# Block boundaries by halves: sums, spreads, roots and slices in another order, and a tile of weights rounded earlier

## The reference, cut to what matters

```python
# first block, each layer
x = x + rms_norm(m, norm_mix_post[l])          # m = merged @ w_out, the mixer's last product
h = rms_norm(x, norm_ffn_pre[l])
f = (silu(h @ w_gate) * (h @ w_up)) @ w_down
x = x + rms_norm(f, norm_ffn_post[l])
# second block, each layer
x = x + gt1 * (mix @ w_out)
h = rmsnorm(x, g_ffn[l]) * (1 + sc2) + sh2
x = x + gt2 * ((silu(h @ w1) * (h @ w3)) @ w2)
```

## Time and profile before

| | us |
|---|---|
| median of 3 runs | 3113.05 |
| lowest and highest | 3111.66, 3120.28 |
| the profiled execution: its time | 3113.11 |
| its span, first to last instruction | 3111.3 |
| PE busy in it | 3041.8 (98%) |
| PEld, DVE, ACT, POOL busy | 2573.5, 1409.4, 1369.7, 1344.3 |
| mean granted TensorE clock | 0.994 |

### The profile page before, as it was taken

How to read it: one execution, slowest core, us unless ns; L and a number is a source line. 1 busy time by engine, 2 the same in 40 slices (tenths; PEclk the granted TensorE clock), 3 DMA queues, 4 the chain that set the end, 5 groups by cost and what they waited for, 6 DMA issues and landing times. The chain is left out here.

```text
span 3111.3 us, 46651 instructions
## 1 busy us (share of the span) xinstructions
PE 3041.8 (98%) x16812; PEld 2573.5 (83%) x16812; DVE 1409.4 (45%) x2710; ACT 1369.7 (44%) x2215; POOL 1344.3 (43%) x715
## 2 busy tenths in 40 slices
PE   9999999999999999999999999999999999999999
PEld 7788888888887788888888886778888867788888
DVE  5754336555416744445655424953211149532111
ACT  6866554322227765564322224554222245642222
POOL 3333334444453333335344453544444535444454
PEclk9999999999999999999999999999999999999999
DMA  3222223366532122223366523211333332113332
GB/s 134 68 78 92 91 89 115 98 204 202 181 108 77 65 84 84 89 91 135 97 207 197 175 97 104 75 62 55 101 101 108 109 110 69 64 60 101 101 108 101
DMA packets 93609, 333.48 MB, mean 107 GB/s; under 512 B 10864, under 2 KB 12080, under 8 KB 93232
## 3 DMA queue, kind: packets, MB, share of 16 engines
q1 hardware_dynamic: 91760, 325.52, 31.6%
q10 hardware_dynamic: 1728, 6.36, 0.5%
HBM read 329.69 MB, written 8.44 MB: 109 GB/s over the span
## 5 line engine op out<-in xcount | busy, mean ns | idle before, releaser
L462 POOL TENSOR_TENSOR wLo<-wring,wHi 128x1024 fp32r<-128x1024 f32 x466 | 1115.0, 2394 | 1528.9 <-ACT wHi L440 1528.6
L510 PE MATMUL psG<-hHi,wHi 128*128 128x512 f32 (+1 forms) x2960 | 1121.1, 379 | 8.1 <-POOL wLo L462 4.9
L510 PE MATMUL psG<-hLo,wHi 128*128 128x512 f32 (+1 forms) x2960 | 1104.9, 373 | 4.0 <-POOL hLo L595 3.8
L510 PE MATMUL psG<-hHi,wLo 128*128 128x512 f32 (+1 forms) x2960 | 1103.6, 373 | 0.0
L440 ACT ACTIVATE wHi<-wring 128x1024 fp32r<-128x1024 f32 x466 | 491.3, 1055 | 824.7 <-PE psG L510 795.1
L510 PEld LDWEIGHTS psG<-hHi,wHi 128*128 128x128 f32 x2960 | 561.0, 190 | 105.2 <-issue 28.8
L510 PEld LDWEIGHTS psG<-hLo,wHi 128*128 128x128 f32 x2960 | 560.8, 189 | 84.6 <-POOL hLo L595 10.2
L510 PEld LDWEIGHTS psG<-hHi,wLo 128*128 128x128 f32 x2960 | 561.3, 190 | 71.5 <-issue 0.5
L510 PE MATMUL psG<-hidHi,wHi 128*128 128x512 f32 x704 | 267.8, 380 | 0.1
L510 PE MATMUL psG<-hidHi,wLo 128*128 128x512 f32 x704 | 266.8, 379 | 0.0
L510 PE MATMUL psG<-hidLo,wHi 128*128 128x512 f32 x704 | 266.8, 379 | 0.0
(11 more groups left out here) (394 smaller groups left out, 3737.9 us busy)
## 6 DMA issues: line engine op xcount, KB each, us to landing
wring<-in_w SPq DMA_DIRECT2D x474, 512.0 KB, 3.5
modw<-in_wmod SPq DMA_DIRECT2D x96, 512.0 KB, 4.1
head_raw<-in_w SPq DMA_DIRECT2D x16, 512.0 KB, 5.2
e_copies<-e_rows ACTq DMA_DIRECT2D x8, 512.0 KB
T_tab<-e_copies SPq DMA_DIRECT2D x4, 1024.0 KB, 5.4
mask<-in_mask SPq DMA_DIRECT2D x2, 1536.0 KB, 6.0
xin_sb<-in_x SPq DMA_DIRECT2D x4, 512.0 KB, 5.3
e_copies<-e_rows ACTq DMA_DIRECT2D x8, 256.0 KB
```

The source lines that it names most:

```text
L462: pool.tensor_tensor(wLo[:, home(c), :, :], wring[:, home(c), :, :], wHi[:, home(c), :, :], ALU.subtract).then_inc(w_cut[c % RING], 1)
L510: mm = pe.matmul(out, w[:, k, :], r(j), start=start and j == 0 and n == 0, stop=stop and j == len(kts) - 1 and n == 2)
```

## The change

Only the order of steps changes, and three dummy matmuls go. In the first block:

- PE: the spread of N2 for half 0 stands ahead of `out_half(1, 5)`. The spread of N3 for half 0 comes after feature 4 of `out_half(1, 7)` and no longer behind all of it. All sums of N2 for half 1 but the last stand in one group after `out_half(1, 7)`. `keep_awake(pe, 3)` is gone. The spread of N3 for half 1 comes one feature earlier.
- ACT and DVE: two tiles of `normed_half(0)` and `high_half(0)` come before the copy and the square of `out_half(1, 7)`. The root and the inverse of N2 for half 1 come later in their streams, behind tile 4 and tile 5. DVE norms four tiles of half 1, not one, ahead of the first `head_hid`.

In the second block:

- ACT, POOL and SP: chunk `CH2_WR + 1` is rounded behind `out6`, right after chunk `CH2_WR`, and its rest is made ahead of the last kept tile's. The load of chunk `CH2_GU + 1` waits for `out7` itself.
- PE: the sums for half 0 stand in two groups (six tiles, two tiles), no longer one by one between the rest tiles. The last sums of half 1 come after feature 1 of the first SwiGLU tile and not after feature 3, and their spread comes before the second SwiGLU tile.
- DVE: four tiles of half 1 are scaled, not two, ahead of the first `head_hid`.

```diff
@@ first block, PE
                     out_half(1, 4, 4)
-                    out_half(1, 5, 0, 2)
                     half_spread(pe, t_N2[0], 0, 1)
-                    out_half(1, 5, 2)
+                    out_half(1, 5)
                     out_half(1, 6)
                     x_sums_of(0, range(5))
                     out_half(1, 7, 0, 2)
                     x_sums_of(0, range(5, KT))
-                    out_sums(1, range(3, KT - 2))
-                    out_half(1, 7, 2)
+                    out_half(1, 7, 2, 5)
                     half_spread(pe, t_N3[0], 0, 2)
-                    out_sums(1, (KT - 2,))
-                    keep_awake(pe, 3)
+                    out_half(1, 7, 5)
+                    out_sums(1, range(3, KT - 1))
                     head(0, 0, 0, 0, 2, h_done(1))
                     out_sums(1, (KT - 1,))
                     head(0, 0, 0, 2, KT, h_done(1))
...
-                    head(0, 1, 1, 0, 4)
+                    head(0, 1, 1, 0, 3)
                     half_spread(pe, t_N3[1], 1, 4)
-                    head(0, 1, 1, 4)
+                    head(0, 1, 1, 3)
@@ first block, ACT
                     half_root(act, t_N3[0])
+                    high_half(0, range(2))
                     out_square(1, 7)
-                    high_half(0, range(3))
+                    high_half(0, range(2, 5))
                     half_root(act, t_N2[1])
-                    high_half(0, range(3, KT))
+                    high_half(0, range(5, KT))
@@ first block, DVE
                     half_inverse(dve, t_N3[0], 10)
+                    normed_half(0, range(2))
                     out_copy(1, 7)
-                    normed_half(0, range(3))
+                    normed_half(0, range(2, 6))
                     half_inverse(dve, t_N2[1], 11)
-                    normed_half(0, range(3, KT))
+                    normed_half(0, range(6, KT))
                     out_scaled(1, range(KT))
                     half_inverse(dve, t_N3[1], 12)
-                    normed_half(1, range(1))
+                    normed_half(1, range(4))
                     head_hid(0, 0)
-                    normed_half(1, range(1, KT))
+                    normed_half(1, range(4, KT))
@@ second block, SP
-                    for c in range(23, CH2_GU + AHEAD):
+                    for c in range(23, CH2_GU + 1):
                         chunk(c)
+                    sp.wait_ge(*G.is_full(g[f"out{KT - 1}"]))
+                    load_chunk(sp, w, l, CH2_GU + 1)
@@ second block, PE
                     for j in range(KT):
                         rest_tile(0, j)
-                        if j >= 3:
-                            rest_sums(0, (j - 3,))
                     rest_tile(1, 0)
                     rest_tile(1, 1)
-                    rest_sums(0, (KT - 3, KT - 2))
+                    rest_sums(0, range(KT - 2))
                     rest_tile(1, 2)
-                    rest_sums(0, (KT - 1,)).then_inc(T.filled(t_N2[0]), 1)
+                    rest_sums(0, (KT - 2, KT - 1)).then_inc(T.filled(t_N2[0]), 1)
...
-                    head_gemm(pe, g_GU2, 0, 0, 0, words2, h_done(1), 0, 4)
+                    head_gemm(pe, g_GU2, 0, 0, 0, words2, h_done(1), 0, 2)
                     rest_sums(1, range(5, KT)).then_inc(T.filled(t_N2[1]), 1)
-                    head_gemm(pe, g_GU2, 0, 0, 0, words2, h_done(1), 4, KT)
+                    head_gemm(pe, g_GU2, 0, 0, 0, words2, h_done(1), 2, KT)
+                    half_spread(pe, t_N2[1], 1, 4)
                     head_gemm(pe, g_GU2, 0, 0, 1, words2)
-                    half_spread(pe, t_N2[1], 1, 4)
@@ second block, ACT
                         for j in OUT_AT.get(s - 1, ()):
-                            follow(act, CH2_WO + j, g[f"out{j}"])
+                            if j < KT - 1:
+                                follow(act, CH2_WO + j, g[f"out{j}"])
+                            if j == KT - 2:
+                                cut_high(act, CH2_WR + 1)
@@ second block, POOL
                         for j in OUT_AT.get(s - 1, ()):
-                            cut_rest(pool, CH2_WO + j + AHEAD)
+                            if j < KT - 1:
+                                cut_rest(pool, CH2_WO + j + AHEAD)
+                            if j == KT - 2:
+                                cut_rest(pool, CH2_WR + 1)
@@ second block, DVE
-                    scaled_half(1, range(2))
+                    scaled_half(1, range(4))
                     head_hid(0, 0)
-                    scaled_half(1, range(2, KT))
+                    scaled_half(1, range(4, KT))
```

More of the change, by code:

```diff
@@ L2238, in _ @@
                         pe.wait_ge(*G.is_read(g["sa", qt]))
+                    words2 = head_hi, head_lo
                     for j in range(KT):
                         rest_tile(0, j)
-                        if j >= 3:
-                            rest_sums(0, (j - 3,))
                     rest_tile(1, 0)
                     rest_tile(1, 1)
-                    rest_sums(0, (KT - 3, KT - 2))
+                    rest_sums(0, range(KT - 2))
                     rest_tile(1, 2)
-                    rest_sums(0, (KT - 1,)).then_inc(T.filled(t_N2[0]), 1)
+                    rest_sums(0, (KT - 2, KT - 1)).then_inc(T.filled(t_N2[0]), 1)
                     rest_tile(1, 3)
@@ L2254, in _ @@
                     rest_sums(1, range(5))
-                    words2 = head_hi, head_lo
-                    head_gemm(pe, g_GU2, 0, 0, 0, words2, h_done(1), 0, 4)
+                    head_gemm(pe, g_GU2, 0, 0, 0, words2, h_done(1), 0, 2)
                     rest_sums(1, range(5, KT)).then_inc(T.filled(t_N2[1]), 1)
-                    head_gemm(pe, g_GU2, 0, 0, 0, words2, h_done(1), 4, KT)
+                    head_gemm(pe, g_GU2, 0, 0, 0, words2, h_done(1), 2, KT)
+                    half_spread(pe, t_N2[1], 1, 4)
                     head_gemm(pe, g_GU2, 0, 0, 1, words2)
-                    half_spread(pe, t_N2[1], 1, 4)
                     head_gemm(pe, g_GU2, 0, 1, 0, words2)
```

## The result

The changed kernel takes 3096.40 us (median of 4 runs, 3095.95 to 3096.79), the kernel before 3113.43 us in the same batch (3111.66 to 3120.28). The ratio over all these runs is 0.9941, 95% interval 0.9929 to 0.9954, so 0.6% less; the medians lie 17.0 us (0.55%) apart, where 15.6 us had been forecast. The profiled execution of after took 3096.55 us, its span is 3094.8.

The account below looks back on a forecast made before the run. PE, busy 98% of the span, bounds the kernel, so time is won only where it waits, issues useless work or runs at the lower clock. 2 x (3.64 - 0.1) + 5.26 + 3.3 = 15.6 us gave 3097.5 us, range 3093.5 to 3109.

Parts of the forecast that it names:

- Spread of N3: First block, half 0: with 9 matmuls after the sums, the spread starts at 566.46, 1.28 us earlier, and nothing waits.
- Walk to the next tile: First block, half 0: following the feeder chain, the next SwiGLU tile starts at 575.11, against 578.75, winning 3.64 us.
- Half 1 of the first block: First block: a 1.4 us wait moves to feature 4, a clock fall is likely again; taken as -0.1 us.
- The other end: First block, half 1: the tile ends at about 594.45, against 595.52, with 1.07 us as the alternative to -0.1.
- Spread of N2, half 0: First block: this spread moves two features ahead and is worth nothing; a late inverse would cost about 0.1 us.
- Second block, half 0: Waits for weights and squares go, five groups of sums fewer; the spread starts at 2125.20, not 2128.07: 2.87 us.
- Second block, the rest: Feeders shift, half 1's sums and spread come earlier: 5.26 us won in layer 0, 3.3 in layer 1.
- Everything else: Outside the changed places: PE is the bound behind them, so nothing takes the gain back; no loss counted.
- the clock falls all the same: Rival, both blocks: clock falls remain, leaving 10.5 us won, 3102.5 us, or 3104.5 with layer 1 too; 25%.
- Switching is not saved: Rival, second block: fewer groups of sums save nothing, leaving 12.3 us won, 3100.8 us; 5%.
- little comes through: Rival: DVE's new order gives back what it wins; about 6.6 us won, 3106.5 us, within 0.3%; 20%.
- Slower: Rival, second block: ACT's double rounding makes the mixed tile late, holding PE some 12 us a layer; 5%.

Follow-up runs that it names:

- e10: The changed kernel with only PE's spread of N3 for half 0 in the first block back behind the whole of `out_half(1, 7)`; 3097.88 us.
- e3: The changed kernel with the three dummy matmuls put back ahead of the first head product in the first block; 3097.53 us.
- e2: Only the second block's part of the change, with the first block as in the kernel before; 3103.58 us.
- e9: e4 with ScalarE's rounding of the first two SwiGLU chunks of the first block moved behind the third silu; 3093.86 us.
- e8: The changed kernel with two spreads of N2 back in their old places: half 0 in the first block, half 1 in the second; 3099.78 us.
- e6: The changed kernel with the second block's sums for half 0 again in seven groups between the tiles, weights still early; 3102.91 us.
- e7: The changed kernel with the second block's earlier rounding of the second rest chunk taken back on SP, ScalarE and GpSimd; 3101.69 us.
- e1: Only the first block's part of the change, with the second block as in the kernel before; 3104.24 us.
- e4: The changed kernel with the first block's `head_hid` behind all eight normed tiles of half 1, and all eight high parts ahead of the second silu; 3093.70 us.
- e11: The changed kernel run again unchanged, in the batch of e9 and e10; 3097.81 us.

## Why the prediction was right, point by point

The mechanisms hold, and the time is right to 1.1 us (3097.5 against 3096.4), the difference to 1.4 (15.6 against 17.0). That closeness is in part luck: in the profiled execution the four places won 18.5 us, 2.9 more than the sum, and everything else, put at nothing, lost 1.9. By its own steps:

- **Spread of N3.** 567.03 - 0.63 = 566.40; forecast 566.46. Of the 3.73 us that follow, e10 shows 0.6 to be this step's.
- **Walk to the next tile.** Spread of N2 at 574.84 - 0.63 = 574.21 (574.3), tile at 575.02 (575.11): 3.73 us for 3.64, and 3.87 in layer 1. That the removed dummies are no part of it, e3 shows. That some 1.5 us of it are clock is an estimate from the spacing of before's matmuls; that the fall belongs to the old order is borne out, since in all four old-order layers profiled (before, e2) the clock fell here, and in none of the 24 with the new order or parts of it.
- **Half 1 of the first block: the term that was mis-sized.** The wait came where I had put it, on ACT's high part of feature 4: 1.42 us between two starts, 1.31 more than a product's 0.11, for 1.4. Then I added a clock fall as likely and took -0.1 us. It did not come: +0.75 in layer 0, +0.81 in layer 1 (4.68 less 3.87). The other end, 1.07, was nearer. Nearly all of this is the missing fall and not the order. Layer 1 of e2 has the old order, had by chance no fall in half 1, and won 0.69 us there against before's execution; that leaves 0.1 us for the new order at the same clock. Across the nine kernels that keep a wait in half 1, a fall follows in 9 of 18 layers and costs 1.2 to 1.6 us; the term's mean over executions is then about 0.8 - 0.7 = 0.1 us, not far from mine, while in a given execution it is +0.8 or anything from -0.4 to -0.8. What I had called likely is even odds. e9 shows what was left there: 1.5 us a layer.
- **Spread of N2, half 0:** worth nothing, confirmed by e8.
- **Second block, half 0.** Spread at 2117.89 + 7.28 (what had been won up to this place) = 2125.17 for 2125.20. The parts as I gave them, 1.04 of wait for weights, 0.46 for squares and 1.67 of switching, make 3.17 and not the 2.87 that I counted as a whole: one switch of 0.33 stands in the first two as well. e6 measures the switches at 1.67 us and e7 the rounding at 1.70. Both lie wholly ahead of the spread, which starts at 2121.39 in e6 and 2120.14 in e7, 1.67 and 1.68 us later than in after once what each had won before (5.45, 6.71) is added. Together they would make 3.35, but the spread is 2.90 earlier than in before: they overlap by 0.45. That is the price of one group, and in before one stood between the first tiles and the late one, so that PE reached its wait 0.45 us later. By the Trainium skill's rule on weight loads that are pulled ahead (TensorE: Matmul & The Clock Gate, Part 2, step-by-step) alone, e6 would have lost nothing; it lost 1.67, so at this switch the row was the right guide.
- **Second block, the rest.** The tile at 2131.50 against 2144.07 is 12.57, less 7.28: 5.29 us for 5.26. A further 0.42 came in half 1, which I had given no gain. Layer 1 gave 3.61 for 3.3. I had put the 1.95 us between the layers down to the clock; e1 bears that out (1.88, and 2.02 the other way round). What the step did not see is that it hangs on the early spread (e8, 1.2 us).
- **Everything else: costed at nothing, lost 1.9 us.** 0.66 of it went before the first layer's work settles, which lies between 1.09 lost and 0.64 won over all kernels here with the same code: scatter. And 1.01 went at the closing norm of layer 0 in the first block, where the clock stood at its lower level under the norm's spread and before it fell only behind it (1.16 against 2.07 us, shown above). No edit touches that norm. The spread took 1.97 to 2.08 us in all twelve kernels with the new first order, and the norm lost 0.8 to 1.3; in e2, whose first block is that of before, it took 1.77 and the norm lost 0.7. So the execution of before that I had measured from was the lucky one at this place; whether the new order adds anything is not settled. The sentence that nothing takes the gain back, since PE is the bound behind the places, left the clock out.

Of the rivals, *the clock falls all the same* was half true: not behind half 0 and not in the second block, but behind half 1 in half of the layers. In the two profiled executions of the changed code it cost 0 and 1.41 us. *Switching is not saved* is rejected by e6, *little comes through* by e1 and e2. *Slower* would have needed ACT's double rounding to hold PE; the mixed tile came in time, and e7, without it, is slower.

## What to carry to other kernels

Where one engine fills 98% of the span, time lies in the few places where it waits, and each is worth its wait plus whatever the clock does behind it: cost the two as separate terms, and the second with both ends, since the same code shows it in one execution and not in another. Ask of every tile that moves ahead of a buffer-freeing instruction who needs that buffer, and cost edits that meet on one queue together (e8). Where medians differ by less than they scatter, compare the traces matmul by matmul.

## What the runs showed of the hardware that was not expected

- VectorE's 128x256 cast and subtraction take 0.29 to 0.5 us with GpSimd idle, and up to 2.04 and 2.49 when begun during GpSimd's 128x1024 subtraction of 2.5 us: they end 0.2 to 0.3 us behind it (e4, e9). The trace of before had it already, where nobody waited for it; the same subtraction in the earlier trace rows took 0.92:

```profile
595.26 2.55 DVE L1836 TENSOR_TENSOR hidLo<-hid_tmp,hidHi 128x256 fp32r<-128x256 f32 x1
```

- The same code at the same place is followed by a stretch at 0.50 in one execution and not in another: e1 and before in the second block, after and e11 in the first. A short stretch (3.4 us) at the lower level costs 1.2 to 1.6 us, the long one of the second block 1.9 to 2.0.
- A group of 128x64 sums set apart between 128x256 products costs PE 0.33 us more than the same sums in company: five of them 1.67 us in either layer (e6).
- Behind a wait of 3.0 to 3.2 us the closing norm's eight spread matmuls took 1.16 us in one of fourteen executions, at the upper level of the clock, and 1.77 to 2.08 in the others.
